# A two-block transformer on one core: attention masks made during the convolution, projections that wait per row block, paired mod sums, another DVE order in gate/up, and a last norm by pairs of tiles

## The chip, the cores and the metric

The kernel is one launch on one core of a Trainium2 chip. The metric is the device time of a launch in microseconds (us); three runs of the kernel before took 3088.89, 3094.58 and 3098.93 us, median 3094.58. Engines: PE (TensorE, matmuls; PEld is its weight load), DVE (VectorE), ACT (ScalarE), POOL (GpSimd), and SP, which here only issues DMAs.

## The reference, cut to what matters

Two blocks over 1024 tokens of width 1024, all f32. The parts that the change touches:

```python
def second_block(x, c, ctx, c_ctx, w_mod, b_mod, ...):
    mod = silu(c) @ w_mod + b_mod            # 6 rows of 1024; the same of c_ctx, 2 rows of use
    hx = rmsnorm(x, norm1_g) * (1 + sc1) + sh1
    q, k, v, u, b, c, ga, gc = split(hx @ w_in)
    # attention over a window of 128 keys at either side and 256 context keys, with sinks
    logits = concat([where(valid, q @ k.T * scale, NEG_INF), q @ k_ctx.T * scale, sink])
    o = softmax(logits) @ v
    # short convolution over tokens, zeros at the edges
    z = c * u
    y = b * (w[0] * z[t - 1] + w[1] * z[t] + w[2] * z[t + 1])
    merged = sigmoid(ga) * (o @ w_proj_attn) + sigmoid(gc) * (y @ w_proj_conv)
    x = x + g1 * (merged @ w_out)
    x = x + g2 * expert_choice_moe(rmsnorm(x, norm2_g) * (1 + sc2) + sh2)   # 16 experts
    return rmsnorm(x, final_norm_g)
```

The first block's feed-forward part, `(silu(xn @ w_gate) * (xn @ w_up)) @ w_down` with 2816 hidden features, is touched too, since the mod rows of the second block are computed beside it.

## The kernel before, in words

**How a product is made.** An f32 operand is split into a high part (`w_high` and its like, ACT) and a low part (`w_low`, DVE: the value less its high part), and `mm3` multiplies high by high, high by low and low by high, three matmuls of 128x512 for one k (a slice of 128 of the contraction). `feat_group` is one output of 128 features by 512 tokens: eight k, 24 matmuls into one of the 8 PSUM banks.

**Order.** Every engine runs a list of functions, one stage after another, strictly in the order in which they are written (`run_pe`, `run_dve` and so on). Engines are tied by semaphores: `did` and `landed` count an event up, `wait_ge` waits for one. `bank` hands out PSUM banks in turn and waits for the event that freed the bank before. There is no planner; what is written first on an engine goes first.

**Gate/up (`ffn_*`).** 22 iterations c; each makes 128 gate and 128 up features for all tokens by seven Strassen-like products P1 P6 P2 P7 P5 P4 P3 of 12 matmuls. P3 adds into the bank of P5 after DVE has read C22 out of it (`gu_product`, `gu_c22`). In iteration c, ACT and DVE also split the weights for c + 1 (`gu_high`, `gu_low`).

**Mod rows.** DVE multiplies 48 quarters of `w_mod` (512 columns, 2 k each) by silu(c) per partition and adds them up in `accs` (`mod_add`); chunks 0 to 3 have two rows (c and c_ctx), 4 to 11 one. Two quarters go into each iteration 1 to 8, four into each of 9 to 16 (`mod_at`). PE then sums over the partitions with a column of ones (`mod_sum_pe`), ACT copies the row out, POOL stores it. The loads of the next quarters (`mod_load`) are on SP's queue, in turn with the gate/up weights.

**Conv and attention.** `conv_*` makes u, c and b for eight feature tiles m and DVE forms y in four passes of 1024 columns; POOL stores y. `mix_*` runs 64 steps s of two heads: PE scores (`qk2`), DVE scale, mask and row maximum (`max2`), ACT exp, PE transposes (`turn2`), ACT and DVE copies, and after four steps PE the product with the values (`values2`) and the row sums. Between them PE does the gate projection, 4 k per step (`gate_part`), into bank 6. The additive masks, the ones and the sinks are made by POOL at the start of `mix_pool`; the masks lie where the conv's second half of buffers (`yb`) lies, so POOL first waits until y is stored.

**Projections and out.** `proj_pe` starts a group when the low part of all eight k is there. `out2_part` starts when the merged rows are all split. **Last norm.** SP loads eight tiles of 128 tokens; ACT squares and sums in halves of 512, DVE makes the mean and the inverse for four tiles at a time and then scales all tiles.

## Time and profile before

| | |
|---|---|
| median of three runs | 3094.58 us (3088.89 to 3098.93) |
| profiled execution: time, span | 3099.16 us, 3097.3 us |
| PE busy | 2868.4 us (93%), 14050 matmuls |
| DVE, ACT, POOL busy | 1721.3 (56%), 1307.7 (42%), 513.9 us (17%) |
| granted PE clock, mean | 0.968 |
| gate/up iterations 0 to 21 | about 550 to 1010 us |
| conv, attention, projections, out and router | about 1310 to 1692, to 2128, to 2319, to 2500 us |
| experts, last norm | to 3058, to 3097 us |

All times below are microseconds from the start of the span, unless marked ns. A row of the instructions in order of time reads: start, duration, engine, line, operation, output<-inputs, form, how many, and in brackets the idle time before with what ended it. Rows that come from a helper all have the helper's line: L125 is any matmul, L128 a transpose, L131 any activation, L134 a tensor_tensor, L140 a scalar_tensor_tensor, L143 a multiply-and-reduce.

### The profile page before, as it was taken

To read this page: it belongs to the slowest core of one execution; us is meant where nothing else is said; L and a number is where in the kernel's file an instruction comes from. 1 tells how busy PE (TensorE), PEld (TensorE's weight loads), DVE (VectorE), ACT (ScalarE), POOL (GpSimd) and SP (SyncE) were. 2 spreads that over 40 slices of the span, in tenths; PEclk is the share of its full clock that TensorE was granted. 3 is DMA by queue.
4 is the path that set the end of the run, shared out by engine and by line. 5 is a ranking of instruction groups with operands and counts; after the bars stand their busy time and mean duration, and the time that the engine had idled before them with its cause. 6 is when DMAs were issued, how large, how long until landed. Compare 5 with 4: busy or idle time off the path is not lost.

```text
span 3097.3 us, 34772 instructions
## 1 busy us (share of the span) xinstructions
PE 2868.4 (93%) x14050; PEld 2276.3 (73%) x14050; DVE 1721.3 (56%) x2349; ACT 1307.7 (42%) x1831; POOL 513.9 (17%) x429
## 2 busy tenths in 40 slices
PE   5999988999999899899998999999999579999994
PEld 4777766777778788788886676666787368888883
DVE  3344534666775234743322555554345679999994
ACT  5344433332333223211111666664223357777773
POOL 1011112445444000321000111111000200000000
PEclk9999989999999999899999999999999789999997
DMA  3210121334654521231211111113334569999994
GB/s 117 68 42 28 42 101 70 116 109 143 175 156 142 192 85 48 71 89 52 70 60 41 38 42 42 42 38 136 99 106 163 217 234 392 391 398 397 398 386 137
DMA packets 239477, 439.29 MB, mean 142 GB/s; under 512 B 27421, under 2 KB 134053, under 8 KB 238805
## 3 DMA queue, kind: packets, MB, share of 16 engines
q1 hardware_dynamic: 217184, 359.69, 33.1%
q0 software_dynamic: 21984, 77.33, 7.4%
q8 instruction: 112, 1.84, 0.2%
q14 instruction: 49, 0.39, 0.0%
q10 hardware_dynamic: 148, 0.04, 0.0%
HBM read 383.43 MB, written 53.58 MB: 141 GB/s over the span
## 4 chain that ended last, share of the span: by engine, by line
PE 84%; DVE 7%; ACT 3%; DMA 2%; issue 2%; POOL 0%; SPq 0%; ACTq 0%; DVEq 0%; POOLq 0%
PE PS L125 79%; PE PS L128 5%; DVE m L134 3%; ACT m L131 3%; DVE m L140 2%; DMA m<-in_w_down_dram 1%; ACT L131 0%; DMA xa_scratch<-m,small 0%; DVE m L176 0%; DVE m L179 0%; DVE m L173 0%; DVE m L143 0%; DMA mod_scratch<-m 0%; DVE m L137 0%; DMA m<-xa_scratch 0%
## 5 line engine op out<-in xcount | busy, mean ns | idle before, releaser
L125 PE MATMUL PS<-m,m 128*128 128x512 f32 (+4 forms) x12234 | 2669.6, 391 | 79.6 <-DVE m L134 53.1
L125 PEld LDWEIGHTS PS<-m,m 128*128 128x128 f32 (+2 forms) x12234 | 2066.3, 185 | 609.2 <-issue 120.7
L131 ACT ACTIVATE m<-m 128x2048 fp32r<-128x2048 f32 (+4 forms) x614 | 708.1, 1167 | 913.1 <-PE PS L125 449.8
L134 DVE TENSOR_TENSOR m<-m,m 128x2048 fp32r<-128x2048 f32 (+5 forms) x574 | 837.5, 1480 | 429.0 <-ACT m L131 400.5
L131 ACT ACTIVATE m<-PS 128x512 f32<-128x512 f32 (+4 forms) x503 | 280.5, 578 | 569.6 <-PE PS L125 384.4
L134 DVE TENSOR_TENSOR m<-PS,m 128x512 fp32r<-128x512 f32 (+1 forms) x360 | 237.2, 686 | 374.8 <-PE PS L125 322.5
L134 POOL TENSOR_TENSOR m<-m,m 128x512 f32<-128x512 f32 (+3 forms) x166 | 253.4, 1529 | 686.4 <-DVE small L143 218.7
L128 PE MATMUL PS<-ident,m 128*128 128x128 f32 (+1 forms) x1592 | 231.2, 286 | 107.1 <-DVE m L149 36.0
L128 PEld LDWEIGHTS PS<-ident,m 128*128 128x128 f32 (+1 forms) x1592 | 198.8, 147 | 146.5 <-DVE m L149 36.2
L131 ACT ACTIVATE m<-m,small 128x640 f32<-128x640 f32 (+5 forms) x200 | 158.1, 792 | 206.7 <-DVE small L137 141.2
L143 DVE CUSTOM_DVE_ANT_0 m<-PS,m 128x640 f32<-128x640 f32 (+4 forms) x192 | 146.5, 775 | 127.1 <-PE PS L125 118.9
L149 DVE COPY m<-PS 128x512 f32<-128x512 f32 (+1 forms) x176 | 107.0, 617 | 143.4 <-PE PS L128 102.9
L140 DVE SCALAR_TENSOR_TENSOR m<-m,small,m 128x512 f32<-128x512 f32 (+1 forms) x154 | 143.6, 963 | 1.5
L131 ACT ACT_TABLE_LOAD x91 | 116.8, 1283 | 30.4 <-DVE small L137 24.9
L140 DVE SCALAR_TENSOR_TENSOR m<-m,vecT,m 128x512 fp32r<-128x512 f32 (+3 forms) x96 | 64.0, 723 | 48.2 <-ACT m L131 47.3
L134 POOL TENSOR_TENSOR m<-m 128x512 f32<-128x512 f32 x52 | 75.1, 1447 | 27.7 <-DMA m<-in_w_gate_up_dram 17.7
L185 POOL DMA_INDIRECT m<-xh_scratch,small x16 | 19.6, 1224 | 303.3 <-PE PS L128 283.8
L185 POOL DMA_INDIRECT xa_scratch<-m,small x16 | 25.1, 1569 | 243.1 <-DVE m L140 243.1
L134 DVE TENSOR_TENSOR small<-small 128x8 f32<-128x8 f32 (+4 forms) x52 | 10.3, 201 | 99.2 <-ACT small L131 63.9
L131 ACT ACTIVATE m<-m,vecT 128x512 fp32r<-128x512 f32 (+2 forms) x80 | 41.1, 595 | 39.9 <-PE PS L125 39.9
L134 POOL TENSOR_TENSOR m<-ident,small 128x1024 f32<-128x1024 f32 x16 | 43.3, 2707 | 33.4 <-DVE small L155 33.4
L182 POOL DMA_DIRECT2D y_scratch<-m x8 | 4.3, 542 | 259.8 <-DVE m L134 259.8
(78 smaller groups left out, 467.0 us busy)
## 6 DMA issues: line engine op xcount, KB each, us to landing
m<-in_w_exp_gate_dram SPq DMA_DIRECT2D x64, 1024.0 KB, 9.7
m<-in_w_exp_up_dram SPq DMA_DIRECT2D x64, 1024.0 KB, 9.9
m<-in_w_exp_down_dram SPq DMA_DIRECT2D x64, 1024.0 KB, 9.4
m<-in_w_mod_dram SPq DMA_DIRECT2D x48, 512.0 KB, 3.7
m<-in_w_gate_up_dram SPq DMA_DIRECT2D x44, 512.0 KB, 5.3
m<-in_w_in_dram SPq DMA_DIRECT2D x41, 512.0 KB, 4.1
m<-in_w_in_dram SPq DMA_DIRECT2D x12, 1024.0 KB, 5.1
h_scratch<-m POOLq DMA_DIRECT2D x22, 512.0 KB, 3.9
```

The costliest lines, as they stand in the source:

```text
L125: return Unsent() if self.e is None else self.e.matmul(o, l, r, start=first, stop=last, **k)
L128: return Unsent() if self.e is None else self.e.transpose(o, i, ident)
L131: return Unsent() if self.e is None else self.e.activation(o, i, fn, **k)
L134: return Unsent() if self.e is None else self.e.tensor_tensor(o, a, b, op)
L140: return Unsent() if self.e is None else self.e.scalar_tensor_tensor(out=o, in0=a, scalar=s, in1=b, op0=op0, op1=op1)
L143: return Unsent() if self.e is None else self.e.tensor_tensor_reduce(**k)
L149: return Unsent() if self.e is None else self.e.tensor_copy(o, i)
L182: return Unsent() if self.e is None else self.e.dma_start(o, i)
L185: return Unsent() if self.e is None else self.e.indirect_dma_start(*a, **k)
```

## The change

- `mod_add`: the second quarter of an iteration is no longer in front of C22. With two quarters it comes last, after C12; with four they stand at the start, after P4's low half, after P3's and last.
- Mod sums: eight pairs (`MOD_PAIRS`) in place of 16 single ones. The sums of a pair go to partitions 0 and 64 of one bank. From chunk 4 on a slot of `accs` is used again four chunks later, not two.
- Masks, ones and sinks are made at the start of `conv_pool`. For that u lies in `sil`, and zb and yb are moved. DVE does the first maximum in the conv, before the four passes of the last tile; ACT loads Exp's table at the conv's end; ACT's wait for the last y moves to the first sigmoid. In step 0 PE does the gate projection's four k in one piece, before the scores of step 1.
- `feat_group` takes a wait per k, which both projections use; `out2_part` waits per k too.
- Last norm: pairs of tiles. ACT squares the even tile, DVE the odd one, each in one pass; the inverse is made per pair. Of the first three pairs ACT scales the even tile and POOL multiplies it by the gain, DVE does the odd one; of the last DVE does both. The root's table is loaded while PE is in the last product.

```diff
-        def feat_group(pe, n, mt, h, rhs, sem, key, freed_by):
+        def feat_group(pe, n, mt, h, rhs, sem, key, freed_by, ready=None):
...
             for k in range(8):
+                if ready:
+                    pe.wait_ge(*ready(k))
                 r = rhs(k, h)
...
+        MOD_PAIRS = [((c, 0), (c, 1)) for c in range(4)] + [((c, 0), (c + 1, 0)) for c in range(4, 12, 2)]
+        def acc_slot(c, j):
+            return c % 2, j if c < 4 else c // 2 % 2
...
-                pe.matmul(PS[0:1, b, :], one, accs[c % 2][j], True, True).then_inc(*pe.did("mod_sum", c, j))
+        def mod_sum_pe(pe, n):
+            b = pe.bank("mod_row", *MOD_PAIRS[n][1])
+            pe.wait_ge("masks", "one")
+            for a, (c, j) in enumerate(MOD_PAIRS[n]):
                 bank_of["mod_sum", c, j] = b
                 pe.wait_ge("mod_step", c, j)
+                t = pe.matmul(PS[64 * a:64 * a + 1, b, :], one, acc_of(c, j), True, True, skip_group_check=True)
+            t.then_inc(*pe.did("mod_sum", n))
...
                     gu_low(dve, c + 1, P)
-                for q in qs[1:2]:
-                    mod_add(dve, q)
                 gu_c22(dve, c)
                 gu_low(dve, c + 1, "P4")
-                for q in qs[2:3]:
+                for q in qs[1:-2]:
                     mod_add(dve, q)
...
                 gu_low(dve, c + 1, "P3")
+                for q in qs[2:-1]:
+                    mod_add(dve, q)
                 gu_c12(dve, c)
-                for q in qs[3:4]:
+                for q in qs[-1:]:
                     mod_add(dve, q)
...
-        ub = [ar(32, 512), ar(34, 512)]
-        zb = ar(36, 1028)
+        ub = sil
+        zb = ar(37, 1028)
...
-        yb = [ar(144, 1024), ar(148, 1024)]
+        yb = [ar(41.25, 1024), ar(144.5, 1024)]
...
+            act.activation(tab, one, ACT.Exp).then_inc(*act.did("act_table"))
...
                     y = yb[m % 2]
+                    if m == 7:
+                        dve.wait_ge("amask")
+                        dve.wait_ge("sink_in")
+                        max2(dve, 0)
...
         def conv_pool(pool):
+            pool.wait_ge("rope_out", *LAST_ROPE)
+            mix_masks(pool)
...
+                if s == 0:
+                    gate_part(pe, s, 0, 4)
                 if s + 1 < NS2:
                     qk2(pe, s + 1)
-                gate_part(pe, s, 0, 2)
+                if s:
+                    gate_part(pe, s, 0, 2)
...
             for n in range(16):
-                pe.wait_ge("o2_low", n % 2, 7)
-                feat_group(pe, W_PA + n // 2, 0, n % 2, orhs, "p_acc", (n,), ("pa_out", n))
+                feat_group(pe, W_PA + n // 2, 0, n % 2, orhs, "p_acc", (n,), ("pa_out", n), lambda k: ("o2_low", n % 2, k))
...
-                pe.wait_ge("m2_low", 31 if i > 3 else 30)
             for k in range(k0, k1):
...
                 pe.wait_ge("w_low", n)
+                pe.wait_ge("m2_low", 16 + 2 * k + (i > 3))
...
         def final_act(act):
...
+            act.activation(tab, one, ACT.Sqrt).then_inc(*act.did("act_table"))
...
+            for j in range(4):
+                i = 2 * j
+                act.wait_ge(f"x_in{i}", "f")
+                act.wait_ge("act_junk~")
+                act.activation(xf_junk[0], XF[:, i, :], ACT.Square, accum_out=ssum[:, i:i + 1]).then_inc(*act.did("act_junk~", "f", i))
+                root_of(act, ssum[:, i:i + 2], "f", j)
+                if j < 3:
+                    act.wait_ge("rstd", "f", j)
+                    act.activation(XF[:, i, :], XF[:, i, :], ACT.Copy, scale=rs8[:, i:i + 1]).then_inc(*act.did("xf_scaled", i))
...
+                for t in range(i + (j < 3), i + 2):
+                    dve.scalar_tensor_tensor(XF[:, t, :], XF[:, t, :], rs8[:, t:t + 1], fg, ALU.mult, ALU.mult).then_inc(
+                        *dve.did("y_out_f", t))
...
+        def final_pool(pool):
+            pool.wait_ge("fg_in")
+            for i in (0, 2, 4):
+                pool.wait_ge("xf_scaled", i)
+                pool.tensor_tensor(XF[:, i, :], XF[:, i, :], fg, ALU.mult).then_inc(*pool.did("y_out_p", i))
```

DVE in gate/up, iteration 2, from U3 on. First before: L140 rows are the second mod quarter, `m8_57<-PS,m72_121` is C22, `m8_57<-m72_121,PS` C21, `m1_50<-PS,m71_120` C12.

```order
L134 TENSOR_TENSOR m72_121<-PS,m71_120 128x512 [waits s_gu_acc,s_gu_up]
L134 TENSOR_TENSOR m131_180<-m69_118,m130_179 128x512 [waits s_w_high]
L134 TENSOR_TENSOR m139_188<-m67_116,m138_187 128x512 [waits s_w_high]
L140 SCALAR_TENSOR_TENSOR m36_85<-m41_90,small,m36_85 128x512 [waits s_mod_step,s_mod_raw1]
L140 SCALAR_TENSOR_TENSOR m37_86<-m41_90,small,m37_86 128x512 [waits s_mod_step]
L140 SCALAR_TENSOR_TENSOR m36_85<-m41_90,small,m36_85 128x512 [waits s_mod_step]
L140 SCALAR_TENSOR_TENSOR m37_86<-m41_90,small,m37_86 128x512 [waits s_mod_step]
L134 TENSOR_TENSOR m8_57<-PS,m72_121 128x512 [waits s_st0,s_gu_acc,s_gu_up]
L134 TENSOR_TENSOR m133_182<-m149_198,m132_181 128x512 [waits s_w_high]
L134 TENSOR_TENSOR m8_57<-m72_121,PS 128x512 [waits s_gu_acc]
L134 TENSOR_TENSOR m135_184<-m70_119,m134_183 128x512 [waits s_w_high]
L134 TENSOR_TENSOR m1_50<-PS,m71_120 128x512 [waits s_pool_once,s_gu_acc]
```

The same place in the changed kernel:

```order
L134 TENSOR_TENSOR m72_121<-PS,m71_120 128x512 [waits s_gu_acc,s_gu_up]
L134 TENSOR_TENSOR m132_181<-m69_118,m131_180 128x512 [waits s_w_high]
L134 TENSOR_TENSOR m140_189<-m67_116,m139_188 128x512 [waits s_w_high]
L134 TENSOR_TENSOR m8_57<-PS,m72_121 128x512 [waits s_st0,s_gu_acc,s_gu_up]
L134 TENSOR_TENSOR m134_183<-m150_199,m133_182 128x512 [waits s_w_high]
L134 TENSOR_TENSOR m8_57<-m72_121,PS 128x512 [waits s_gu_acc]
L134 TENSOR_TENSOR m136_185<-m70_119,m135_184 128x512 [waits s_w_high]
L134 TENSOR_TENSOR m1_50<-PS,m71_120 128x512 [waits s_pool_once,s_gu_acc]
L140 SCALAR_TENSOR_TENSOR m36_85<-m41_90,small,m36_85 128x512 [waits s_mod_step,s_mod_raw1]
L140 SCALAR_TENSOR_TENSOR m37_86<-m41_90,small,m37_86 128x512 [waits s_mod_step]
L140 SCALAR_TENSOR_TENSOR m36_85<-m41_90,small,m36_85 128x512 [waits s_mod_step]
L140 SCALAR_TENSOR_TENSOR m37_86<-m41_90,small,m37_86 128x512 [waits s_mod_step]
```

The four L140 rows moved from in front of C22 to behind C12.

DVE from the last tile of the conv into the attention. First before: L137 with `vecT`, two L140 and L134 with `m74_123` are the four passes of y, L143 from PS is the maximum.

```order
L134 TENSOR_TENSOR m95_144<-PS,m94_143 128x512 [waits s_out_a,s_uc_acc]
L137 TENSOR_SCALAR m90_139<-m95_144,vecT 128x1024 [waits s_st1,s_cz_out]
L140 SCALAR_TENSOR_TENSOR m90_139<-m95_144,vecT,m90_139 128x1024 [waits s_y_step] x2
L134 TENSOR_TENSOR m90_139<-m90_139,m74_123 128x1024 [waits s_y_step]
L143 ISA m102_151,small<-PS,m99_148 128x512 [waits s_s_acc,s_sink_in,s_amask]
L143 ISA small 128x1
L137 TENSOR_SCALAR small<-small 128x1 [waits s_s_max]
L143 ISA m103_152,small<-PS,m99_148 128x512
L143 ISA small 128x1
L137 TENSOR_SCALAR small<-small 128x1 [waits s_s_max]
L134 TENSOR_TENSOR m129_178<-m149_198,m129_178 128x1024 [waits s_w_high]
```

In the changed kernel:

```order
L134 TENSOR_TENSOR m93_142<-PS,m1_50 128x512 [waits s_out_a,s_uc_acc]
L143 ISA m101_150,small<-PS,m99_148 128x512 [waits s_s_acc,s_sink_in,s_amask]
L143 ISA small 128x1
L137 TENSOR_SCALAR small<-small 128x1 [waits s_s_max]
L143 ISA m102_151,small<-PS,m99_148 128x512
L143 ISA small 128x1
L137 TENSOR_SCALAR small<-small 128x1 [waits s_s_max]
L137 TENSOR_SCALAR m95_144<-m93_142,vecT 128x1024 [waits s_st1,s_cz_out]
L140 SCALAR_TENSOR_TENSOR m95_144<-m93_142,vecT,m95_144 128x1024 [waits s_y_step] x2
L134 TENSOR_TENSOR m95_144<-m95_144,m74_123 128x1024 [waits s_y_step]
L134 TENSOR_TENSOR m130_179<-m150_199,m130_179 128x1024 [waits s_w_high,s_st0]
```

The first maximum (two L143 from PS) stands in front of the four passes, and the second one follows the weights' low half (L134, 128x1024).

PE at the same place, first before, from the second half of the scores of step 0: rows with inputs `m73_122` are scores, those with `m128_177` (`m129_178` in the changed kernel) and m80/m81 gate matmuls, L128 transposes.

```order
L125 MATMUL PS<-m84_133,m73_122 128x256 x2
L125 MATMUL PS<-m82_131,m73_122 128x256 [waits s_s_max]
L125 MATMUL PS<-m82_131,m73_122 128x256
L125 MATMUL PS<-m84_133,m73_122 128x256 x2
L125 MATMUL PS<-m80_129,m128_177 128x512 [waits s_w_low,s_s_acc]
L125 MATMUL PS<-m81_130,m128_177 128x512
L125 MATMUL PS<-m80_129,m128_177 128x512 x2
L125 MATMUL PS<-m81_130,m128_177 128x512
L125 MATMUL PS<-m80_129,m128_177 128x512
L128 MATMUL PS<-ident,m102_151 128x128 [waits s_s_exp]
```

In the changed kernel:

```order
L125 MATMUL PS<-m84_133,m73_122 128x256 x2
L125 MATMUL PS<-m80_129,m129_178 128x512 [waits s_w_low,s_s_acc]
L125 MATMUL PS<-m81_130,m129_178 128x512
L125 MATMUL PS<-m80_129,m129_178 128x512 x2
L125 MATMUL PS<-m81_130,m129_178 128x512
L125 MATMUL PS<-m80_129,m129_178 128x512 x2
L125 MATMUL PS<-m81_130,m129_178 128x512
L125 MATMUL PS<-m80_129,m129_178 128x512 x2
L125 MATMUL PS<-m81_130,m129_178 128x512
L125 MATMUL PS<-m80_129,m129_178 128x512
L125 MATMUL PS<-m82_131,m73_122 128x256 [waits s_s_max]
L125 MATMUL PS<-m82_131,m73_122 128x256
```

Twelve gate matmuls now stand between the scores of step 0 and those of step 1, and the second scores no longer come ahead of them.

## Rows read from the trace of the kernel before

**Rows 1.** The page's chain that ended last, shares of the span.

```profile
PE 84%; DVE 7%; ACT 3%; DMA 2%; issue 2%; POOL 0%; SPq 0%; ACTq 0%; DVEq 0%; POOLq 0%
```

**Rows 2.** Groups by line and form, PE, 566 to 930: busy, mean ns, idle before.

```profile
L125 PE MATMUL PS<-m,m 128*128 128x512 f32 x1456 | 336.9, 391 | 13.7 <-DVE m L134 13.7
L125 PE MATMUL PS<-m,small 128*1 128x512 f32 x32 | 15.7, 591 | 0.0
```

**Rows 3.** Instructions in time, PE, gate/up: start, us, what, [idle before].

```profile
569.04 19.34 PE L125 MATMUL PS<-m,m 128*128 128x512 f32 x84 [2.34 <-DVE m L134]
589.60 19.33 PE L125 MATMUL PS<-m,m 128*128 128x512 f32 x84 [1.22 <-DVE m L134]
...
784.13 1.02 PE L125 MATMUL PS<-m,small 128*1 128x512 f32 x2
785.08 19.34 PE L125 MATMUL PS<-m,m 128*128 128x512 f32 x84
```

**Rows 4.** The same of DVE, iteration 1.

```profile
586.21 2.73 DVE L140 SCALAR_TENSOR_TENSOR m<-m,small,m 128x512 f32<-128x512 f32 x4
588.86 0.68 DVE L134 TENSOR_TENSOR m<-PS,m 128x512 f32<-128x512 f32 x1
...
598.16 0.69 DVE L134 TENSOR_TENSOR m<-PS,m 128x512 f32<-128x512 f32 x1 [4.82 <-PE PS L125]
```

**Rows 5.** Groups by form, PE, 1727.5 to 1732, product with the values.

```profile
L125 PE MATMUL PS<-m,m 128*64 128x512 f32 x16 | 3.7, 598 | 0.0
```

**Rows 6.** Instructions in time, conv's end and attention's start.

```profile
1689.90 0.69 DVE L134 TENSOR_TENSOR m<-PS,m 128x512 f32<-128x512 f32 x1 [4.75 <-PE PS L125]
...
1690.74 1.13 PE L125 MATMUL PS<-m,m 64*128 64x256 f32 x8 [0.88 <-DVE m L134]
...
1694.06 1.22 DVE L134 TENSOR_TENSOR m<-m,m 128x1024 f32<-128x1024 f32 x1
...
1703.54 0.69 DVE L143 CUSTOM_DVE_ANT_0 m<-PS,m 128x512 f32<-128x512 f32 x1 [8.26 <-DMA small<-in_attn_sink_dram]
...
1705.24 4.93 PE L125 MATMUL PS<-m,m 64*128 64x256 f32 x14 [13.37 <-DVE small L143]
...
1708.36 1.23 DVE L134 TENSOR_TENSOR m<-m,m 128x1024 fp32r<-128x1024 f32 x1 [3.01 <-ACT m L131]
...
1713.02 0.73 PEld L125 LDWEIGHTS PS<-m,m 64*128 64x128 f32 x8 [0.36 <-issue]
...
1716.37 2.70 PE L125 MATMUL PS<-m,m 128*128 128x512 f32 x14
```

**Rows 7.** The same, start of the attention projection.

```profile
2128.94 10.85 DVE L134 TENSOR_TENSOR m<-m,m 128x512 fp32r<-128x512 f32 x17
...
2133.89 8.38 PE L125 MATMUL PS<-m,m 128*128 128x512 f32 x27 [5.68 <-DVE m L134]
```

**Rows 8.** One stretch of it: busy of each engine, PEclk, DMA.

```profile
2134.00:2139.00 5.00, 5.00 (x14) 3.96 (x15) 5.00 (x9) 3.64 (x7) 0.00 (x0) 0.59 1.02 412
```

**Rows 9.** Instructions in time, start of the conv projection.

```profile
2224.92 9.71 DVE L134 TENSOR_TENSOR m<-m,m 128x512 fp32r<-128x512 f32 x16
...
2229.87 10.46 PE L125 MATMUL PS<-m,m 128*128 128x512 f32 x37 [6.67 <-DVE m L134]
```

**Rows 10.** The same, start of the out projection.

```profile
2322.93 4.49 DVE L134 TENSOR_TENSOR m<-m,m 128x2048 fp32r<-128x2048 f32 x2 [1.11 <-ACT m L131]
...
2325.28 20.02 PE L125 MATMUL PS<-m,m 128*128 128x512 f32 x80 [3.58 <-DVE m L134]
```

**Rows 11.** The same, DVE, last norm.

```profile
3083.94 9.64 DVE L140 SCALAR_TENSOR_TENSOR m<-m,small,m 128x1024 f32<-128x1024 f32 x8
```

**Rows 12.** The eight loads of the last norm, 3065 to 3069.

```profile
DMA to landing us min/median/max: 3.4/7.6/10.3
```

**Rows 13.** Groups by form, POOL and ACT, 1024 columns, whole run.

```profile
L134 POOL TENSOR_TENSOR m<-m,m 128x1024 f32<-128x1024 f32 x10 | 25.1, 2516 | 106.3 <-DVE m L140 106.3
...
L131 ACT ACTIVATE m<-m,small 128x1024 f32<-128x1024 f32 x10 | 11.5, 1148 | 14.9 <-DVE small L143 14.9
```

More of the change, by code:

```diff
@@ L2978, in final_dve @@
[L2978 to L2988 removed]
+            act.wait_ge("masks", "one")
@@ L3019, in run_pool @@
             moe_pool(pool)
+            final_pool(pool)
         def run_act(act):
```

103 lines of the change are left out of this document (54 added, 49 removed).

## The prediction

> **What bounds the kernel now.** I read the page's chain of waits first: 84% of it is PE, 79% one kind of line, the matmul helper [rows 1]. So time can come only from places where PE waits or does work that can go, and each part of the change is priced there. The next view was busy time in equal stretches: PE is full in most and short in the first half of gate/up, at the start of the attention, at both projections, at the out projection and at the end. Then I read the instructions in order of time at those places.
>
> - Gate/up, first half: PE stops once per iteration, 1.2 to 1.7 us, released by DVE [rows 3]. From 566 to 930 us all its idle time is 13.7 us [rows 2], of which 2.34 lies in iteration 0 [rows 3], where no mod sum is made.
> - Start of the window attention: PE idle 13.37 us [rows 6].
> - The two projections: 5.68 us [rows 7] and 6.67 us [rows 9].
> - The out projection: 3.58 us [rows 10].
> - The last norm: eight DVE passes, 9.64 us, start only when all statistics are made [rows 11].
>
> **The change part by part.** The sum is made against the profiled execution: 3099.16 us, span 3097.3 (PE's and DVE's work lies inside). It is 4.6 us above the median of the three runs, 3094.58; the gain is subtracted from the median too.
>
> A. *mod_add in gate/up.* In iterations 1 to 8 DVE does quarter two (four passes, 2.73 us, 586.21) before C22 (588.86), and P3 on PE waits for C22: PE starts at 589.60 [rows 3, 4], right after. Without it C22 follows P5's end at once, during P4, so the stall goes. Eight stalls are the 13.7 less the 2.34 [rows 2, 3], with 0.3 us of a late store of a mod row at 862 that the longer slot reuse also frees: 11.4 us. The moved passes now sit after C12, where DVE idled 4.82 us before the next U2 (598.16) [rows 4]; 2.73 fits. SP's queue has the next gate/up weights behind the mod load that waits for this quarter, about 3 to 5 us later than now; these weights are for the iteration after the next, an iteration being 20 us, so nothing shows. Iterations 9 to 16 have no stall of this kind and gain none. Bounds: 9 to 11.4.
>
> B. *Mod sums in pairs.* A sum is a 512-column f32 matmul with one column of weights, recorded as two: 16 of them, 32 records, 15.7 us busy [rows 2]; by start times 784.13 to 785.08 one takes 0.95 [rows 3], in all 15.2. PE has no slack here, so it is on the path. The instructions stay 16, but the two of a pair write partitions 0 and 64 of one bank. The nearest row is the product with the values: 16 records, eight matmuls that write partition halves in turn, 3.7 us [rows 5], 0.93 a pair, as long as one alone. So eight pairs cost 7.6 to 7.8 and 7.4 us go. If they don't overlap: 0. I take 7.4, as the row has the same columns and output halves. ACT's copies and POOL's stores keep their number and lie beside PE.
>
> C. *Masks, first maximum and gate matmuls at the attention's start.* Now: DVE takes the last conv product at 1689.90, the conv's four passes end at 1695.28 (1694.06 + 1.22), the store, masks and sinks follow, DVE starts the maximum at 1703.54, PE the second scores at 1705.24 and the third at 1713.02 [rows 6]. After: first scores end at 1691.9 (1690.74 + 1.13). DVE does the maximum at once, 1.7 us as between 1703.54 and 1705.24: 1693.6. Then the four conv passes, 4.7: 1698.3; the weights' low half, 1.23 (1708.36) [rows 6]: 1699.6; the second maximum, 1.7: third scores at 1701.3. PE has twelve gate matmuls (2.8 us), the second scores and eight transposes until about 1697, then waits some 4 us. What PE does up to the third scores is the same work in both, so 1713.0 - 1701.3 = 11.7 us is the gain. Exp's table is loaded in the conv, where ACT idles. The clock may fall in the 4 us: the 14 matmuls of 1705.24 took 4.93 us and the same 14 of 1716.37 2.70 [rows 6], so 2.2 us can be lost. Bounds 7 to 13.4 (the whole idle); I take 11.
>
> The same rows bear on the clock: the short one at 1705.24 follows 13 us of idle. The Trainium skill (TensorE: Matmul & The Clock Gate, Part 4: PE-mode transpose) says transposes don't count as PE being busy; by that rule the eight transposes before the new wait add to it and the 2.2 us are lost for certain.
>
> D. *Projections wait per k.* First: DVE makes low halves from 2128.94 at 17 in 10.85, 0.61 each; PE starts after the eighth, 2133.89 [rows 7]. After: it starts after the first, 2129.6, and uses 0.69 per k (three matmuls of 0.23, 84 in 19.34 [rows 3]), slower than DVE, so it doesn't starve: 4.3 us. Also 27 matmuls took 8.38 us [rows 7], 0.31 each, at a granted clock of 0.59 from 2134 to 2139 [rows 8], between the 1.2 and 2.4 GHz levels; at 0.23 they take 6.2. With 1.4 us of idle in place of 5.7 I expect the full level: 2.2 more. Against that, the third weight piece is loaded while the big transfers of this stage run and PE comes for it 6 us sooner: 0.5 off. 6.0 us, bounds 2 to 6.5. Second: 16 low halves from 2224.92 in 9.71, PE at 2229.87 with 37 matmuls in 10.46 against 8.5 [rows 9]: 4.3 + 2.0 = 6.3, bounds 4 to 6.3; its next weights are ready at about 2239 and needed at 2247.
>
> E. *Out projection.* The per-k wait changes nothing. At 2325.28 PE goes on after DVE's weight passes that start at 2322.93 [rows 10]: it has done k 0 to 3, and the second piece of w_out is late, because ACT makes its high half only after the last projection matmul. The 3.58 us stay. 0, bounds 0 to 0.5.
>
> F. *Last norm.* Eight loads are issued from 3065.2 to 3068.5 and land 3.4 (first) to 10.3 us (last) later, median 7.6 [rows 12]: by that tile 1 is there at about 3070, tile 3 at 3074, tile 7 at 3079. A pair costs DVE 1.2 for a square and sum (same columns as a pass of 9.64 / 8 [rows 11]), some 0.7 for mean, root and inverse (ACT in between), 1.2 for its own tile. ACT's square or scale is 1.15 [rows 13], below that. Pairs end at 3073, 3077.2, 3080.5, and the last, with two passes, at 3084.9. POOL multiplies three tiles at 2.5 [rows 13], the last from 3080.3 to 3083, before DVE's last. Today DVE ends at 3093.58 [rows 11]: 8.7 less, and I give 0.4 back as the last four stores now queue behind each other. The root's table load moves under the last product. 8.3 us, bounds 5 to 9.
>
> DVE's passes of 1024 columns that share time with POOL's work elsewhere are the doubt in F. The Trainium skill (GPSIMD Engine Reference, Key points) says POOL shares its SBUF interfaces with VectorE and collides with DVE instructions of two SBUF inputs, which these are; no row here shows this pair side by side.
>
> Sum: 11.4 + 7.4 + 11 + 6.0 + 6.3 + 0 + 8.3 = 50.4 us. 3099.2 - 50.4 = 3048.8 for the profiled execution, 3044 for the median.
>
> **Rivals.**
> 1. The paired sums don't overlap (B = 0): 3051.6. For: weights of one column, not 64. Against: [rows 5].
> 2. The projections' gain is given back: weights and gate tiles follow PE's pace through SP's queue, and when PE starts earlier the third piece arrives when it did. D = 0: 3056.5. For: big transfers run just then. Against: PE needs it only 22 us after its start, and the load is released by DVE, which also is earlier.
> 3. The low clock at the attention's start, and more idle there: C = 7 to 9: 3047 to 3048.
> 4. Slower. DVE enters the attention with the conv's last passes behind its first maximum, 4 us late; if the lag stays, PE waits at the scores of each of 63 steps. From 60 / 63 = 0.95 us a step this outweighs all, and at 1.3 the time is 3126. Against: today DVE starts 13 us late, and the row at 1716.37 already has no idle [rows 6].
>
> **How the numbers follow.** Forecast as summed 0.66 (own range 3038 to 3051, from the bounds of C, D and F and 4 us of run scatter), rival 1 0.10, rival 2 0.12, rival 3 0.09, rival 4 0.03. The range 3036 to 3060 leaves out rival 4, part of rival 2 and the tails. A difference under 0.3% (9 us) can't be told from none here. All cases but rival 4 are over 30 us faster: faster 0.96, same 0.01, slower 0.03.
>
> **What would show it.** A: no PE idle before P3 in iterations 1 to 8, an iteration at 19.3 to 20.3 us. B: a pair's four records start to next matmul 0.95, not 1.8. C: third scores 11 us after the last conv matmul's end, not 23. D: PE's first projection matmul 1.5 us after its last sums, clock full. E: 3.6 us idle remains. F: from the first load's issue to the end 24 us in place of 32. The prediction is wrong if PE's total idle shrinks by less than 30 us, or if a new idle over 5 us stands at the third weight piece or in the attention's steps.

## The result and the profile after

The changed kernel takes 3061.6 us in the median of four runs (3057.39 to 3062.72), the kernel before 3092.61 beside it: ratio 0.9895, 95% interval 0.9875 to 0.9915, some 31 us faster. The forecast was 3044.0, 50.4 us below before: 17.6 us off, and 1.6 outside its range. Timed again later the pair stood at 3060.04 and 3098.3 (0.9878, 0.9863 to 0.9893). The runs of the kernel before spread over 3088 to 3099 us, those of the changed one over 3057 to 3063.

Profiled executions compare best: 3099.16 before, 3061.53 after (span 3059.5), 37.6 us less. Each stage is measured between two events that it has in both traces:

| stage, between which PE starts | before | after | gained | forecast |
|---|---|---|---|---|
| gate/up, from the restart after the 2.34 us of iteration 0 to the last mod sum's end | 358.20 | 339.57 | 18.6 | A + B 18.8 |
| attention, first scores to last row sums (2127.14 before, 2095.30 after) | 436.40 | 426.59 | 9.8 | C 11 |
| from there to the end of the conv projection | 194.56 | 192.79 | 1.8 | D 12.3 |
| from there through the out projection, to the router's wait for the copy at L149 (2429.96, 2394.76) | 108.26 | 106.67 | 1.6 | E 0 |
| last norm, first load's issue to the span's end | 32.06 | 29.64 | 2.4 | F 8.3 |

The other 3.4 us lie ahead of that restart (1.5) and between the last mod sum and the conv (1.9), where the change does nothing. So the terms were 12.8 us too large in sum; the other 4.8 are that the profiled execution of before lay 4.6 above its median and that of the changed kernel on its own, and rounding.

One execution isn't the whole of it. Nine profiled executions, two of the changed kernel and seven of edits that leave these stages alone, have the same code from the last row sums to the end of the conv projection: they take 186.5 to 192.8 us there (median 188.1), so against before's 194.56 the gain is 1.8 to 8.0 us, and the table shows the least. The attention gains 8.2 to 9.9 in the ten executions that have its code.

Gate/up by line and form, after, the stretch and columns of [rows 2] moved to 564 to 910:

```profile
L125 PE MATMUL PS<-m,m 128*128 128x512 f32 x1459 | 335.5, 390 | 4.0 <-DVE m L134 4.0
L125 PE MATMUL PS<-m,small 128*1 128x512 f32 x32 | 8.2, 590 | 0.0
```

The 13.7 us of idle are 4.0, of which 2.34 is iteration 0 and the rest new waits of 0.25 to 0.40 us in iterations 12 to 16. The 32 records of the sums are busy 8.2 us in place of 15.7.

The attention's start in order of time, PE, after, against [rows 6]:

```profile
1668.71 5.29 PE L125 MATMUL PS<-m,m 64*128 64x256 f32 x28 [0.88 <-DVE m L134]
1673.92 1.09 PE L128 MATMUL PS<-ident,m 128*128 128x128 f32 x8
1679.13 4.23 PE L125 MATMUL PS<-m,m 64*128 64x256 f32 x14 [4.11 <-DVE small L143]
```

The scores of the first step, twelve gate matmuls and the second step's scores are one row; the third step's start 10.42 us after the first (1679.13 - 1668.71), where they started 22.3 after it. The 13.37 us of idle are 4.11, and the 14 matmuls behind them still slow (2.7 us in the steps that follow).

The projections, PE, after, against [rows 7, 9, 10]:

```profile
2095.30 1.08 PE L125 MATMUL PS<-m,m 128*64 128x512 f32 x4 [1.12 <-POOL m L134]
2097.93 22.04 PE L125 MATMUL PS<-m,m 128*128 128x512 f32 x96 [1.55 <-DVE m L134]
2124.10 68.09 PE L125 MATMUL PS<-m,m 128*128 128x512 f32 x288 [4.13 <-DVE m L134]
2195.28 92.81 PE L125 MATMUL PS<-m,m 128*128 128x512 f32 x396 [3.08 <-DVE m L134]
2291.67 30.22 PE L125 MATMUL PS<-m,m 128*128 128x512 f32 x132 [3.58 <-DVE m L134]
```

PE starts 1.55 us after its last sums, not 5.68, and does 96 matmuls, the four groups of the first two weight pieces, at 0.23 us each. Then it stands 4.13 us. The third piece, in order of time on SP, ACT, DVE and PE:

```profile
2094.21 15.96 SPq L182 DMA_DIRECT2D m<-sa_scratch  x6
...
2110.21 2.58 SPq L182 DMA_DIRECT2D m<-in_w_proj_attn_dram  x4
2121.74 1.06 ACT L131 ACTIVATE m<-m 128x1024 fp32r<-128x1024 f32 x1 [15.91 <-DMA m<-in_w_proj_attn_dram]
2122.82 1.22 DVE L134 TENSOR_TENSOR m<-m,m 128x1024 fp32r<-128x1024 f32 x1 [13.01 <-ACT m L131]
...
2124.10 8.26 PE L125 MATMUL PS<-m,m 128*128 128x512 f32 x24 [4.13 <-DVE m L134]
```

Its four transfers stand in SP's queue behind six gate tiles' loads and go out at 2110.21; ACT gets the piece 11.5 us later. The next one takes 6.8 (2125.64 to 2132.41). The wait stands in all nine executions, 1.25 to 4.13 us long. The granted clock behind the stall, in equal stretches (PE, PEld, DVE, ACT, POOL busy, then the clock and the transfers' share):

```profile
2107.00:2117.00 10.00, 10.00 (x46) 8.28 (x45) 2.25 (x3) 0.00 (x0) 0.00 (x0) 1.00 1.04 397
...
2124.00:2126.00 2.00, 1.90 (x5) 1.51 (x6) 1.25 (x3) 0.00 (x0) 0.00 (x0) 0.50 0.10 36
2126.00:2128.00 2.00, 2.00 (x6) 1.61 (x5) 0.00 (x0) 0.00 (x0) 0.00 (x0) 0.50 0.81 277
```

The transfer engines are full up to 2117, and PE goes on at 1.2 GHz: 24 matmuls in 8.26 us in place of 5.5.

The last norm, all engines in order of time, after:

```profile
3036.57 1.28 DVE L140 SCALAR_TENSOR_TENSOR m<-m,small,m 128x1024 f32<-128x1024 f32 x1
...
3037.86 2.34 POOL L134 TENSOR_TENSOR m<-m,m 128x1024 f32<-128x1024 f32 x1 [12.60 <-ACT m L131]
3038.40 2.89 DVE L143 CUSTOM_DVE_ANT_0 m<-m 128x1024 f32<-128x1024 f32 x1 [0.55 <-DMA m<-xa_scratch]
...
3043.27 3.39 POOL L134 TENSOR_TENSOR m<-m,m 128x1024 f32<-128x1024 f32 x1 [3.06 <-ACT m L131]
...
3044.58 2.11 DVE L137 TENSOR_SCALAR small<-small 128x2 f32<-128x2 f32 x1
...
3052.27 2.48 DVE L140 SCALAR_TENSOR_TENSOR m<-m,small,m 128x1024 f32<-128x1024 f32 x2
```

A DVE pass of two columns takes 2.11 us, and ends at 3046.69, when POOL's product does (3043.27 + 3.39 = 3046.66). A square that takes 1.23 alone takes 2.89 and ends 1.1 us after POOL's. Pairs follow at 5.1 to 5.5 us.

### The profile page after: what moved, and what is told of

It is laid out like the page before. It is cut to its first block, busy times and chain, and to the rows that moved or that the text cites. A ratio compares the mean times of both kernels' runs of the same rounds, so it can differ in the third digit from the quotient of the medians.

```text
span 3059.5 us, 34754 instructions
## 1 busy us (share of the span) xinstructions
PE 2856.7 (93%) x14050; PEld 2273.1 (74%) x14050; DVE 1759.6 (58%) x2356; ACT 1303.1 (43%) x1814; POOL 532.9 (17%) x432
## 4 chain that ended last, share of the span: by engine, by line
PE 85%; DVE 7%; ACT 3%; DMA 2%; issue 2%; POOL 1%; SPq 0%; ACTq 0%; DVEq 0%; POOLq 0%
PE PS L125 80%; PE PS L128 5%; DVE m L134 3%; ACT m L131 2%; DVE m L140 1%; DMA m<-in_w_down_dram 1%; POOL m L134 1%; DVE m L143 1%; ACT L131 0%; DVE m L176 0%; DVE m L179 0%; DVE m L173 0%; DMA m<-in_w_proj_attn_dram 0%; DMA m<-xa_scratch 0%; DMA m<-in_w_proj_conv_dram 0%
## 5 line engine op out<-in xcount | busy, mean ns | idle before, releaser
L125 PE MATMUL PS<-m,m 128*128 128x512 f32 (+4 forms) x12234 | 2665.8, 391 | 56.2 <-DVE m L134 38.3
L134 DVE TENSOR_TENSOR m<-m,m 128x2048 fp32r<-128x2048 f32 (+5 forms) x574 | 851.1, 1503 | 445.7 <-ACT m L131 417.2
L131 ACT ACTIVATE m<-m 128x2048 fp32r<-128x2048 f32 (+5 forms) x602 | 701.3, 1180 | 929.6 <-PE PS L125 437.9
L134 DVE TENSOR_TENSOR m<-PS,m 128x512 fp32r<-128x512 f32 (+1 forms) x360 | 236.6, 684 | 300.1 <-PE PS L125 249.6
L134 POOL TENSOR_TENSOR m<-m,m 128x512 f32<-128x512 f32 (+3 forms) x169 | 273.0, 1618 | 674.6 <-DVE small L143 219.3
L128 PE MATMUL PS<-ident,m 128*128 128x128 f32 (+1 forms) x1592 | 229.7, 284 | 107.2 <-DVE m L149 36.0
L128 PEld LDWEIGHTS PS<-ident,m 128*128 128x128 f32 (+1 forms) x1592 | 197.3, 147 | 146.5 <-DVE m L149 36.2
L131 ACT ACTIVATE m<-m,small 128x640 f32<-128x640 f32 (+5 forms) x203 | 161.6, 797 | 221.1 <-DVE small L137 154.9
L143 DVE CUSTOM_DVE_ANT_0 m<-PS,m 128x640 f32<-128x640 f32 (+4 forms) x192 | 146.4, 775 | 120.1 <-PE PS L125 120.1
L149 DVE COPY m<-PS 128x512 f32<-128x512 f32 (+1 forms) x176 | 106.9, 617 | 144.2 <-PE PS L128 103.6
L140 DVE SCALAR_TENSOR_TENSOR m<-m,small,m 128x512 f32<-128x512 f32 (+1 forms) x151 | 158.7, 1078 | 1.7
L140 DVE SCALAR_TENSOR_TENSOR m<-m,vecT,m 128x512 fp32r<-128x512 f32 (+3 forms) x96 | 64.0, 722 | 48.0 <-ACT m L131 47.1
L134 POOL TENSOR_TENSOR m<-m 128x512 f32<-128x512 f32 x52 | 74.9, 1444 | 27.7 <-DMA m<-in_w_gate_up_dram 17.8
L134 DVE TENSOR_TENSOR small<-small 128x8 f32<-128x8 f32 (+4 forms) x50 | 9.9, 202 | 76.0 <-ACT small L131 63.9
L134 POOL TENSOR_TENSOR m<-ident,small 128x1024 f32<-128x1024 f32 x16 | 43.3, 2707 | 33.4 <-DVE small L155 33.4
```

The costliest lines, as they stand in the source:

```text
L125: return Unsent() if self.e is None else self.e.matmul(o, l, r, start=first, stop=last, **k)
L128: return Unsent() if self.e is None else self.e.transpose(o, i, ident)
L131: return Unsent() if self.e is None else self.e.activation(o, i, fn, **k)
L134: return Unsent() if self.e is None else self.e.tensor_tensor(o, a, b, op)
L140: return Unsent() if self.e is None else self.e.scalar_tensor_tensor(out=o, in0=a, scalar=s, in1=b, op0=op0, op1=op1)
L143: return Unsent() if self.e is None else self.e.tensor_tensor_reduce(**k)
```

## Experiments

Each is an edit of the changed kernel unless it says otherwise. The runs were taken in four groups, each with the kernel before beside it (medians 3098.30, 3096.43, 3096.02 and 3097.52 us), but only the first group, that of the projections, had the changed kernel in it too. So elsewhere the stage that an edit changes is compared, or the distance to the kernel before.

### The projections

The yardstick of the group is the changed kernel itself; the kernel before took 3098.30 us beside it.

> The changed kernel as it is, timed beside the others of this group as their yardstick. All theories: 3058 to 3063 us, 29 to 34 us below the kernel before.

3060.04 us (3058.8 to 3060.85). Of the nine executions this is the odd one: the low clock fell in the first two pieces (96 matmuls in 24.86 us, where the other eight took 22.0), so the third piece made PE wait 1.25 us only; the conv projection's idle was 2.16.

Per-k waits undone:

```
-  feat_group(..., orhs, ..., lambda k: ("o2_low", n % 2, k))
+  feat_group(..., orhs, ..., lambda k: ("o2_low", n % 2, 7))
-  ... lambda k: ("y_low", n % 2, k))
+  ... lambda k: ("y_low", n % 2, 7))
```

> The changed kernel, but the first group of each projection half waits for all eight low halves again, as before the change. Theory G (given back): in the changed kernel PE's earlier start in the attention projection (31.84 us ahead of before) only moves it into the third weight piece, which comes when it came before: 4.13 us of idle and then 24 matmuls in 8.26 us at a granted clock of 0.50 instead of 5.5 (2.7 lost). So without the per-k waits the attention projection costs the same (within 1 us), and the conv projection 2.6 us more: 1.5 to 3 us slower than the changed kernel, and no idle over 1 us before the third piece. Theory F (the forecast): 12.3 us slower than the changed kernel.

3064.53 us (3062.93 to 3065.72), 4.5 above the yardstick. PE, in order of time:

```profile
2103.81 89.00 PE L125 MATMUL PS<-m,m 128*128 128x512 f32 x384 [5.77 <-DVE m L134]
2199.64 91.61 PE L125 MATMUL PS<-m,m 128*128 128x512 f32 x396 [6.83 <-DVE m L134]
```

No wait at the third piece. From the last row sums the attention projection takes 95.85 us, as it does with the per-k waits (96.89 and, in the yardstick, 94.33). So in the attention projection the gain had been given back. The conv projection takes 98.4 us, as before the change, and with the per-k waits 95.9 and 93.8: there part of the gain stays.

SP issues each projection weight piece one piece earlier:

```
 for n in range(32):
-    if n and n < 16 and n % 2 == 0: w_load(sp, W_PA + n // 2 + 1)
-    if n >= 16 and n % 4 == 0:      w_load(sp, W_PC + (n - 16) // 4 + 1)
+    if n < 16 and n % 2 == 0:       w_load(sp, W_PA + n // 2 + 2)
+    if n in (16, 20, 24):           w_load(sp, W_PC + (n - 16) // 4 + 2)
     gate_load(sp, n + 4)
```

> The changed kernel, but SP issues each projection weight piece one piece earlier: the third of the attention projection before the gate tiles of groups 4 and 5 (its raw buffer is free since the attention), and so on to the first piece of the out projection. Theory Q (the piece is late because its load stands behind a gate tile's wait in SP's queue): it is issued at about 2097 instead of 2110, lies there by 2110 even at the shared rate, ACT and DVE split it in 2.3 us after PE's fourth group, so the idle of 4.13 and the 2.7 us of low clock go: 6.8 us; the conv projection's first piece is split sooner, so its 3.08 us of idle becomes about 2: in all 7 to 8.5 us faster than the changed kernel, about 3054. Theory S (the rate of the transfers alone decides, since 16 queues are 97 to 104% busy from 2097 to 2117): the y load and the rows are then done later and the piece saves less than 3 us; or the second piece comes late instead.

3051.32 us (3048.87 to 3055.3), 8.7 below the yardstick:

```profile
2098.46 4.03 SPq L182 DMA_DIRECT2D m<-in_w_proj_attn_dram  x4
...
2100.36 87.30 PE L125 MATMUL PS<-m,m 128*128 128x512 f32 x384 [1.55 <-DVE m L134]
...
2119.42 1.06 ACT L131 ACTIVATE m<-m 128x1024 fp32r<-128x1024 f32 x1 [11.17 <-DMA m<-in_w_proj_attn_dram]
...
2189.19 90.00 PE L125 MATMUL PS<-m,m 128*128 128x512 f32 x396 [1.53 <-DVE m L134]
```

All 384 matmuls stand in one row. The piece took 21 us from issue to ACT, and was there in time because it was issued 0.7 us after the last row sums (2097.72), not 14.9 (2110.21 - 2095.30). Theories Q and S are both half right: the issue decides, and the shared rate is why a late issue costs so much.

POOL issues the load of y and the rows only when the third piece has landed:

```
+ pool.wait_ge(f"w_raw{W_PA % 2}", W_PA + 2)
  pool.dma_start(yraw, ...)
```

> The changed kernel, but POOL issues the load of y (and the four row loads behind it) only when the third weight piece of the attention projection has landed; SP's order is as in the changed kernel, so the piece is issued at about 2110 still. Theory S (shared rate): the piece lands in 6.8 us, as the later ones do (2125.64 to 2132.41), not in 11.5, is split by about 2119.4, and PE needs it at 2120: the idle of 4.13 and the low clock after it go, 6 to 7 us faster than the changed kernel. Theory Q (queue order alone): the landing stays over 10 us and the time is the changed kernel's. If y then comes late for the conv projection (needed about 95 us later) a new idle would stand there; not expected.

3067.89 us (3064.58 to 3074.72), 7.9 slower than the yardstick:

```profile
2115.24 2.59 SPq L182 DMA_DIRECT2D m<-in_w_proj_attn_dram  x4
...
2120.22 1.06 ACT L131 ACTIVATE m<-m 128x1024 fp32r<-128x1024 f32 x1 [12.18 <-DMA m<-in_w_proj_attn_dram]
...
2126.13 2.67 SPq L182 DMA_DIRECT2D m<-in_w_proj_attn_dram  x4
...
2145.36 1.06 ACT L131 ACTIVATE m<-m 128x1024 fp32r<-128x1024 f32 x1 [24.08 <-DMA m<-in_w_proj_attn_dram]
...
2147.82 2.47 PE L125 MATMUL PS<-m,m 128*128 128x512 f32 x5 [11.94 <-DVE m L134]
```

The third piece takes 5.0 us and no longer makes PE wait, as theory S said. But y's 4 MB and four row loads then meet the fourth, which takes 19.2, and PE stands 11.94 us. I had looked for harm only at y's own reader.

The earlier loads alone, in the kernel before:

> The kernel before, with only SP's earlier issue of the projection weight pieces (as in loads_early); its projections still wait for all eight low halves. In the kernel before no piece was late, so theory Q/S (the pieces were hidden, and become the bound only when PE starts per k) gives no gain: within 2 us of the kernel before; the stalls of 5.7 and 6.7 us at the two projections stay. If early pieces were worth something by themselves, as their 8.7 us in the changed kernel could also be read, the time would be 6 to 9 us below the kernel before.

3097.22 us against 3096.02, ratio 1.000 (0.999 to 1.0009). Nothing. Early loads without early matmuls give 0. Per-k waits without early loads give -0.8 to 1.7 in the attention projection and 2.6 to 6.4 in the conv's, over the nine executions. Both together give, from the last row sums to the end of the conv projection, 98.51 - 91.53 + (96.05 - 89.94) = 13.1 us against before, where 12.3 were forecast. (Those are the two projections' ends, counted from the row sums and from each other: before 96.05 and 98.51, loads early 89.94 and 91.53.)

### The last norm

POOL out, DVE does both products of a pair and still a square:

```
 final_act:  - act.activation(XF[:, i, :], XF[:, i, :], ACT.Copy, scale=rs8[:, i:i + 1])
 final_dve:  - for t in range(i + (j < 3), i + 2):
             + for t in range(i, i + 2):
 final_pool: - pool.tensor_tensor(XF[:, i, :], XF[:, i, :], fg, ALU.mult)
```

> The changed kernel, but in the last norm DVE does both final products of a pair and POOL and ACT's scaling do none; DVE still squares the odd tile. Theory P (DVE and POOL don't run these passes at the same time: in the changed kernel DVE's 2-column TENSOR_SCALAR takes 2.11 us in place of 0.17, and a square 2.89 in place of 1.23, each ending when POOL's product ends): a pair costs DVE 1.2 + 0.7 + 2.6 = 4.5 us in place of 5.1 to 5.5, no 2-column pass is over 0.3 us, and the end is 1.5 to 2.5 us sooner than in the changed kernel, although DVE has three products more. Theory H (no such exclusion; the long rows are waits for data): DVE gets 3 x 1.28 us more work and the end is 3.8 us later.

3057.19 us (3054.34 to 3058.88). From the first load's issue to the end 25.5 us, 4.1 less than with POOL's help:

```profile
3042.37 2.48 DVE L140 SCALAR_TENSOR_TENSOR m<-m,small,m 128x1024 f32<-128x1024 f32 x2
...
3044.77 1.22 DVE L143 CUSTOM_DVE_ANT_0 m<-m 128x1024 f32<-128x1024 f32 x1
...
3046.10 0.17 DVE L137 TENSOR_SCALAR small<-small 128x2 f32<-128x2 f32 x1
...
3046.74 2.48 DVE L140 SCALAR_TENSOR_TENSOR m<-m,small,m 128x1024 f32<-128x1024 f32 x2
```

The small pass is 0.17 again, the square 1.22, a pair 4.37 (3046.74 - 3042.37). Theory P holds: with three more products on DVE the norm is faster. The edit takes ACT's scaling out along with POOL's product. But in the changed kernel ACT's scaling and square were over by 3044.2, and the small pass ended with POOL's product, 2.5 us later.

On top of that edit ACT squares both tiles of a pair, and DVE does only small passes and products:

```
 final_act:  + act.activation(xf_junk[1], XF[:, i + 1, :], ACT.Square, accum_out=ssum[:, i + 1:i + 2])
 final_dve:  - dve.tensor_tensor_reduce(out=xf_junk[1], in0=XF[:, i + 1, :], in1=XF[:, i + 1, :], ...)
```

> The changed kernel, but in the last norm ACT squares both tiles of a pair and DVE does both products; POOL does nothing. Theory P: DVE's pair is 0.7 of small passes and 2.6 of products = 3.3 us, ACT's squares 2.4, so from the first tile's landing: first products 2.7 us later, four pairs to 3.3 + 13.2: the end 5 to 6.5 us sooner than in the changed kernel. Theory H: the transfers or ACT's handshakes bound the norm, and the gain stays under 3 us.

3057.11 us (3052.51 to 3058.15); 24.7 us from issue to end, 5.0 less than the changed kernel. DVE ends at 3050.24, but the span ends 6.06 us later, where it was 3.72 in the kernel before: the last load already shares the transfer engines with the first stores (ACT waits for it until 3045.94, 14.3 us after the first issue), and by my reading the stores bound the rest; no run separates them.

### Gate/up

The two sums of a pair write partition 0 of two banks, and ACT and POOL take the rows from there:

```
- t = pe.matmul(PS[64 * a:64 * a + 1, b, :], one, acc_of(c, j), True, True, ...)
+ b = pe.bank("mod_row", c, j)
+ t = pe.matmul(PS[0:1, b, :], one, acc_of(c, j), True, True, ...)
```

> The changed kernel, but the two mod sums of a pair write partition 0 of two banks in place of partitions 0 and 64 of one. Theory of the forecast: the two no longer overlap, a pair's four records go from 0.95 to 1.9 us, and eight pairs cost 7.4 us more; PE has no slack there, so the time is 7 to 8 us longer. Rival: the pair's short time came from standing next to each other in the program, not from the two column halves of the array: then no difference.

3063.71 us (3061.38 to 3065.59). The four records of a pair take 1.88 in place of 1.03, so standing next to each other isn't enough for them to overlap. The edit changes the output partitions and the banks together; which of the two lets them overlap isn't shown apart. But the stage is only 344.1 us long, 4.6 more than with pairs.

DVE's old order of the mod quarters:

```
  for P in "P7 P5".split(): gu_low(dve, c + 1, P)
+ mod_add(dve, qs[1])
  gu_c22(dve, c); gu_low(dve, c + 1, "P4")
- mod_add(dve, qs[1:-2])
+ mod_add(dve, qs[2])
  gu_c21(dve, c); gu_low(dve, c + 1, "P3")
- mod_add(dve, qs[2:-1])
  gu_c12(dve, c)
- mod_add(dve, qs[-1:])
+ mod_add(dve, qs[3:4])
```

> The changed kernel, but DVE does the mod quarters in gate/up in the old order (the second before C22, the third after P4's low half, the fourth after C12). Theory of the forecast: PE's idle before P3 is back in iterations 1 to 8, 8 x about 1.4 = 11.4 us, and the time 10.5 to 12 us longer; the 0.25 to 0.40 us waits of iterations 9 to 16 of the changed kernel go, 1.7 us, so 9.5 to 11 in all. Rival: with the sums in pairs and the longer reuse of their rows, DVE's order no longer matters: under 3 us.

3069.94 us (3068.99 to 3071.51), and the stage 349.9 us, 10.3 more. The order is thus worth 14.1 us without pairs (358.2 - 344.1) and 10.3 with them, pairs 8.3 without the order and 4.6 with it; together 18.6. Why less than the sum shows when the stage is cut behind the fourth pair of sums (of rows, before), in front of iteration 10:

| | before | pairs, old order (`modorder`) | new order, no pairs (`unpaired`) | changed |
|---|---|---|---|---|
| up to iteration 9 | 195.8 | 192.8 | 182.5 | 179.0 |
| iterations 10 to 17 | 162.4 | 157.1 | 161.6 | 160.6 |

PE in iterations 14 and 15, first in the changed kernel and then in `modorder`:

```profile
826.59 16.62 PE L125 MATMUL PS<-m,m 128*128 128x512 f32 x72
843.61 19.33 PE L125 MATMUL PS<-m,m 128*128 128x512 f32 x84 [0.40 <-DVE m L134]
863.22 3.02 PE L125 MATMUL PS<-m,m 128*128 128x512 f32 x12 [0.27 <-DVE m L134]
...
841.07 38.38 PE L125 MATMUL PS<-m,m 128*128 128x512 f32 x168
```

With two quarters in an iteration the new order brings 13.3 to 13.8 us. With four it costs 3.5 once the sums are paired: PE then waits for DVE in front of P3, and in the old order it doesn't. The old order for iterations 9 to 16 and the new one for 1 to 8 was not tried.

### The attention's start

DVE takes the first maximum after the conv's four passes again, masks stay early (the call `max2(dve, 0)` moves from the last conv tile to the top of `mix_dve`):

> The changed kernel, but DVE takes the attention's first maximum after the last conv tile's four passes again (masks and sinks stay early). Theory M (the 9.9 us at the attention's start come from the masks, which no longer stand between the conv's end and the first maximum, and DVE's sum of passes, 4.7 + 1.7 + 1.2 + 1.7 us, sets the third scores whatever its order): third scores start within 0.5 us of the changed kernel's 10.4 us after the first, idle only moves ahead of the second scores, and the time is within 1.5 us of the changed kernel. Theory N (the order is part of the gain): third scores 3 to 4 us later and the time 3 to 5 us longer.

3062.34 us (3056.49 to 3063.29). Third scores 10.99 us after the first, where the changed kernel's were 10.42, and the attention 427.19 us: 0.6 more in both. (The yardstick, with the changed kernel's own code, needs 428.09, so the 0.6 rests on the third scores.) Most of the idle only moved:

```profile
1668.80 4.22 PE L125 MATMUL PS<-m,m 64*128 64x256 f32 x20 [0.88 <-DVE m L134]
1674.95 1.14 PE L125 MATMUL PS<-m,m 64*128 64x256 f32 x8 [1.93 <-DVE small L143]
1676.01 1.09 PE L128 MATMUL PS<-ident,m 128*128 128x128 f32 x8
1679.79 1.47 PE L125 MATMUL PS<-m,m 64*128 64x256 f32 x8 [2.68 <-DVE small L143]
```

Step 0's gate matmuls where they were before the change (two k after the second scores, one and one between the transposes):

> The changed kernel, but step 0's gate matmuls stand where they did before the change (two after the second scores, one and one between the transposes). Theory M: third scores at the same time, since DVE sets them; within 1.5 us of the changed kernel. Theory N: PE has nothing between first and second scores, idles 1.5 to 2 us there, and ends the attention that much later.

3058.51 us (3055.96 to 3060.03). Third scores 10.42 us after the first, the same to the hundredth, and the attention 425.14 us, 1.5 less: here the low clock fell on 14 matmuls ahead of the third scores, where PE waited anyway. So of term C's parts the moved maximum brings 0.6 and the moved gate matmuls nothing or less. What is left, some 9 us, falls to the early masks and sinks, with Exp's table and ACT's moved wait; no run takes these apart, but in the kernel before it was the sinks' load that ended DVE's wait before the first maximum [rows 6].

Step 1's gate matmuls into the idle before the third scores (`gate_part(pe, 1, 0, 4)` at the end of step 0):

> The changed kernel, but PE does the twelve gate matmuls of step 1 at the end of step 0, before the third scores, where it idles 4.11 us. Theory K (the idle takes any ready work, and the 14 matmuls in 4.23 us at a granted clock of 0.50 to 0.65 are slow because of that idle): idle before the third scores falls to about 1.3 us, the 14 matmuls (now 8) run at full clock, and 2 to 4.4 us are gained. Theory V (DVE's chain of maxima bounds the first steps): PE only waits later, in step 1, and the gain is under 1 us.

3058.32 us (3055.91 to 3059.52). The idle there falls to 1.36 us, and 0.71 and 2.11 us come up in the next step; the attention takes 425.81, 0.8 less. The time is 37.7 us below the kernel before, the yardstick's 38.3: no difference. Theory V fits: DVE's chain sets the pace.

### The out projection, and all together

```
- ROUTE = [("out", 0, 0, 0, 8), ("out", 1, 0, 0, 8), ("out", 2, 0, 0, 8), ...
+ ROUTE = [("out", 0, 0, 0, 4), ("out", 1, 0, 0, 4), ("out", 2, 0, 0, 4),
+          ("out", 0, 0, 4, 8), ("out", 1, 0, 4, 8), ("out", 2, 0, 4, 8), ...
```

> The changed kernel, but the out projection does the first halves (k 0 to 3) of tiles 0, 1 and 2 before the second halves of them, so that the second piece of w_out is needed 36 matmuls (8.3 us) after its start instead of 12. The forecast said that the 3.58 us are this piece, split late by ACT and DVE after the last projection matmul (ready 6.3 us after that). Then the 3.58 us of idle go wholly and 3.6 us are gained, 5 with the low clock that follows the idle in some executions. If instead the m2 halves or x2 tiles were late, the idle moves and the gain is under 1 us.

3052.39 us (3051.26 to 3056.5), 43.6 below the kernel before, where the yardstick is 38.3 below. From the last row sums to the router's wait for the copy at L149 it is 292.44 us against the yardstick's 296.45: 4.0 us are the edit's, the rest scatter. Conv and out projection are one row without a wait:

```profile
2193.51 121.58 PE L125 MATMUL PS<-m,m 128*128 128x512 f32 x528 [3.07 <-DVE m L134]
```

> The changed kernel with the earlier weight loads, the out projection's halves in the other order, step 1's gate matmuls before the third scores, the last norm with ACT's squares and DVE's products, and the first low half of y made before the last attention product's gating. By the parts, against the changed kernel's 3060 in this form: 8.7 (loads, measured) + 5.0 (norm, by the profiles) + 3.6 (out projection) + 2 (gate matmuls) = 19: 3041 us, 3037 to 3045. If the parts eat each other as the per-k waits and the loads did, 3046 to 3050.

3043.65 us (3040.45 to 3044.07), ratio to before 0.9832 (0.9819 to 0.9845); it beats both kernels, the changed one by some 14 us (52.4 below the kernel before, where the yardstick is 38.3 below).

```profile
2097.08 87.29 PE L125 MATMUL PS<-m,m 128*128 128x512 f32 x384 [1.55 <-DVE m L134]
2185.91 0.93 PE L125 MATMUL PS<-m,m 128*128 128x512 f32 x3 [1.54 <-DVE m L134]
2187.01 120.92 PE L125 MATMUL PS<-m,m 128*128 128x512 f32 x525 [0.17 <-DVE m L134]
```

y's first low half ahead of a product brings nothing beyond the early loads (1.54 against 1.53).

## Why the prediction was wrong

The direction was right, and C and E's wait came nearly as forecast, A and B in their sum only. Of the 12.8 us by which the terms were too large in the profiled execution, D holds 10.5 and F 5.9; C adds 1.2, A and B 0.2, and E and the untouched stages give 5.0 back. In the median of the nine executions D gained 6.4 and so holds 5.9. PE's idle time in all shrank by 26.1 us (228.9 to 202.8 by the two pages), less than the 30 that I had set as a sign of being wrong.

- **D, the step that failed.** "... the third weight piece is loaded while the big transfers of this stage run and PE comes for it 6 us sooner: 0.5 off." The start and the clock came as forecast (1.55 us of idle, 96 matmuls in 22.04). Then this piece cost 4.13 + 2.7 = 6.8 us, all of the attention projection's 6.0. Rival 2 described it, at a chance of 0.12. Against it I had written that the load is released by DVE, which also is earlier. It was earlier: SP issues it 14.9 us after the last row sums, where it was 21.0 in the kernel before (2148.16 - 2127.14). But these 6 us put it into the time when y and the rows fill the transfer engines. Before, it was issued when these were nearly done and took 4.8 us (2148.16 to 2153.00), now 11.5. I took the time of its transfer as fixed; [rows 12] had shown eight loads together landing at 3.4 to 10.3. The arithmetic that I left out, here with the changed kernel's numbers: PE wants the piece 24.7 us after the row sums (2119.97), the issue comes at 14.9 and ACT and DVE take 2.4, so the transfer had 7.4 us, and any slowing by the big loads shows. In the conv projection 3.6 of the 4.3 us of idle came, but not the 2.0 of clock: the 396 matmuls took 92.81 us, where before they took 91.83. The idle was 2.1 to 4.0 us in the nine executions, and the 396 matmuls took 90.0 in three of them and 91.6 to 92.9 in the other six. I had counted on full speed behind a shorter idle, and no row of mine showed it.
- **F, the other.** "A pair costs DVE 1.2 for a square and sum ..." and "POOL multiplies three tiles at 2.5 ..., before DVE's last" took DVE and POOL as parallel. Pairs cost 5.1 to 5.5 us, not the 3.1 of my three terms (1.2 + 0.7 + 1.2). I cited the Trainium skill (GPSIMD Engine Reference, Key points) on the interfaces that POOL and DVE share and gave it no price. The Trainium skill says more elsewhere (SBUF — State Buffer, SBUF: two separate sides): the pair of ports that POOL shares with DVE's passes of two SBUF inputs, or in a 2-port mode, is locked for a whole instruction, and the other engine waits. This case's trace agrees for the square (2.89 us, not 1.23), and shows the same of a pass of two columns with one input (2.11, not 0.17). One square and two small passes of DVE were longer by 1.66 + 1.94 + 1.94 = 5.5 us, nearly all of the 5.9 that were lost. It should have been a rival with a price.
- **A and B.** The sum was right (18.6 for 18.8), by luck: two errors cancel. A brings 13.3 to 13.8 us in iterations 1 to 8, more than the 11.4 that I took from the recorded idle, and loses 3.5 in the later ones, of which I had written that they "gain none". So A is 10.3 to 14.1 by itself, B 4.6 to 8.3. Rival 1 is false: 0.96 a pair (627.76 to 628.72).
- **C.** 9.8 for 11, third scores as forecast; the low clock took 1.5 us of it (14 matmuls in 4.23, not 2.7), and 2.2 in the yardstick (4.93). Rival 3 describes this; in the yardstick the attention took 428.09 us, so C was 8.3 there, within rival 3's 7 to 9. The cause was placed too widely: the moved maximum brought 0.6 and the moved gate matmuls nothing.
- **E.** Idle 3.58 us as forecast. That 132 matmuls took 30.22 and not 31.81 is clock: the yardstick, with the same idle, took 31.85. The run `route` shows that the late second piece was the cause, as written: needed later, it leaves no wait.
- **Rival 4** is false: PE stays 31.8 us ahead of before from the attention's third step to its last row sums.
- The range of 3036 to 3060 missed by 1.6 us. It held rival 2 (3056.5), and just so rival 2 with F at the low end of its bounds (3059.8). But F came at 2.4: the bounds of 5 to 9 left the lock out.

## What to carry over

When PE is let in sooner, follow the next two buffers it needs through their queue, and ask what else is in the air when they are issued: an edit that measures nothing by itself (the early loads) and one that brings 2 to 8 us (the per-k waits) were worth 13 together. Before giving POOL a share of DVE's work on SBUF data, ask what DVE does at that time: here the two took turns. Before moving work on an engine, look at every kind of iteration: an order that gained 13.8 us with two quarters lost 3.5 with four. A stall is worth its length plus the slow matmuls behind it, and where the slow ones fall differs between executions of the same kernel.
